# One hybrid encoder layer with 16 experts: bank waits, residual products and x by column halves rearranged, four more expert chunks loaded in the mixing stage

## The chip, the core and the metric

The kernel runs on one core of one Trainium2 chip. The metric is the device time of one execution in microseconds (us); the runs of the kernel before have a median of 499.74 us. TensorE is called PE, VectorE DVE, ScalarE ACT, GpSimd POOL and SyncE SP, as in the profile.

## What is computed

One layer over 256 tokens of width 1024, batch 1, in float32. Three mixers (differential attention, causal pooling, a chunked scan) read one normed projection; their gated sum goes through an output product; then cross attention to 256 memory tokens, and a mixture of 16 experts of which each token takes two.

```python
h = rmsnorm(x, g_mix);  proj = h @ w_in                       # 1024 x 6408
merged = (gates[:, :, 0] * (o_a @ w_branch[0]) + gates[:, :, 1] * (o_b @ w_branch[1])
          + gates[:, :, 2] * (o_c @ w_branch[2]))
x = x + merged @ w_mix_out
x = x + mem_cross_attention(rmsnorm(x, g_xattn), rmsnorm(mem, g_mem), w_xq, w_xkv, w_xo)
x = x + hierarchical_moe(rmsnorm(x, g_moe), ...)              # top-1 group, top-2 expert in it
return rmsnorm(x, g_final)

for e in range(N_EXPERTS):                                    # in hierarchical_moe
    a = jax.nn.silu(hf @ w_gate[e]) * (hf @ w_up[e])
    y = y + comb_dense[:, e:e + 1] * (a @ w_down[e])
```

## The kernel before

Everything is written out by hand: each engine has its own program, and semaphores join them. Nothing is scheduled by a planner.

**Dense stages.** The dense weights come as 80 chunks of up to 512 KB, in the order of the list `BLOCKS`: q, k, v, bcd, xs, pool, z, six gate blocks g0 to g5, the branch products b10 to b21 with the memory keys mka, then m0 and m1 (the output product of the mixers), mkb, xq, mv, xo0, xo1. SP loads chunk n into one of four buffers `raw`. ACT rounds it to fp32r (`wh`, line 622), DVE subtracts that from the raw chunk (`wl`, line 1006), and PE makes three products for each piece (lines 1585 to 1587: high x high, low x high, high x low). `wh` and `wl` have four buffers too. For chunks 0 and 1 the halves are split one by one (`head_hi`, `head_lo`, line 1101), so that the first product can start on half a chunk.

**The start.** x arrives as two DMAs, 128 tokens each with all 1024 columns. PE first multiplies constants (`WARM[0]` = 13 times, line 1596), then transposes the 16 tiles of x (line 1618), where the first tokens' eight come before any of the second tokens'; a transpose of the gains g_mix stands among them (line 1617). Six more warming products follow (line 1592), then chunk 0. ACT and DVE make the high and low parts of the gained columns from the transposes.

**Banks.** Block b of `BLOCKS` sums into the PSUM banks 0 and 1 or 2 and 3 in turn. At a block's first chunk PE waits until both banks of the pair are free (semaphores `free`). In the branch blocks DVE drains a bank by `gates = (gates + 1) * bank` (line 1323) and, outside b10 and b11, adds the result to the sum (line 1326). It waits for its own first instruction, then signals the bank as free with an instruction of its own.

**Experts.** 192 chunks of expert weights (512 KB, two a unit, 96 units) go through 38 buffers (`HOMES`), most of them places that earlier stages no longer need. SP alone issues them, in order. `EARLY` = 9 of them are issued between dense loads, from mka on. The next four go to the part of `gates` that is free once the merged rows are transposed, and are issued after the last dense chunk's load. Later ones wait, each for what frees its place: the products of m1, the last dense chunks, the router's products, and for the places in x the semaphores `x_kept` (PE has copied the residual x into PSUM by products with the identity, `keep_residual`, line 1919) and `moe_rows` (DVE has made the rows for the experts, line 1392). From chunk 38 on each load waits until PE has used up the unit that lay there (lines 1985, 1986 for gate and up, 2003, 2013 and 2039 for down).

**The residual products.** `keep_residual(t, half)` makes a 128x512 product in float32. Two stand after the router's second folded product and before PE waits for the chosen experts, one after the rank products, and one in the first expert's first unit.

**The end.** ACT makes the columns 0 to 511 of the normed output (line 950), DVE the others (line 1578). SP stores tokens 0 to 127 and ACT tokens 128 to 255, 512 KB each.

Of the kernel before, what the change touches and what calls it, by code (L numbers as in the profile page):

```python
# [9 lines left out]
ALU = mybir.AluOpType  # L10
# [3 lines left out]
P = 128  # L14
# [36 lines left out]
EARLY = 9  # L51
RAWG = 16
# [81 lines left out]
WARM = (13, 0, 6, 6, 0, 0, 0, 0)  # L134
# [4 lines left out]
def program(nc, a, out):  # L139
    ctx = ExitStack()  # L140
    with ctx:
# [268 lines left out]
        def _(sp):  # L410
            sp.dma_start(x[:, 0, :], a["x"][0, 0:P, :]).then_inc(s_("x_in0"), 16)
            sp.dma_start(x[:, 1, :], a["x"][0, P:S, :]).then_inc(s_("x_in1"), 16)
# [38 lines left out]
            for n, (name, c, src, kn, cols) in enumerate(CHUNK):  # L451
# [8 lines left out]
                else:  # L460
                    sp.dma_start(dst, src).then_inc(arrived[n % RAW], 16)
                later_parameters(n)
# [23 lines left out]
                if 0 <= n - FIRST["mka"] < EARLY:  # L486
# [3 lines left out]
                    load_chunk(n - FIRST["mka"], n - FIRST["mka"], UNITS)  # L490
            chunks = [2 * u + j for u in ORDER for j in range(2)]
            for at in range(EARLY, len(chunks)):
# [5 lines left out]
                if at < RAWX:  # L498
                    free_by = HOMES[slot][1]
                    if free_by == "mixed":  # L500
                        sp.wait_ge(s_("cols_pe"), COLS["mix"] + 4)
# [32 lines left out]
            sp.wait_ge(s_("final_rows"), 1)  # L534
            sp.wait_ge(s_("final_rows_act"), 1)
            sp.dma_start(out[0, 0:P, :], scaled[:, 0, :]).then_inc(stored, 16)
            sp.wait_ge(stored, 16 * T)
# [64 lines left out]
        def _(act):  # L602
# [87 lines left out]
            act.wait_ge(s_("head_in"), 16)  # L690
            head_hi(0, 0, s_("head_hi"))
# [11 lines left out]
            for t in range(T):  # L703
                square_sum(x[:, t, :], h_ss[:, t:t + 1], hm[:, t, :], s_("sum_squares"))
            for n in range(CHUNKS):
                if n + LEAD < CHUNKS and n != FIRST["mv"]:
                    split(n + LEAD)
                name = BLOCK_AT.get(n)
# [242 lines left out]
            act.wait_ge(s_("final_rows_act"), T)  # L951
            act.wait_ge(s_("final_rows"), T)
            act.dma_start(out[0, P:S, :], scaled[:, 1, :]).then_inc(stored, 16)
# [3 lines left out]
        def _(dve):  # L957
# [138 lines left out]
            def head_lo(n, half):  # L1096
# [3 lines left out]
                dve.wait_ge(hi, n + 1)  # L1100
# [8 lines left out]

            head_lo(0, 0)  # L1110
# [8 lines left out]
            for t in range(T):  # L1119
                mean_square(h_ss[:, t:t + 1], D, h_ss[:, t:t + 1], "h", t)  # L1120
            for n in range(CHUNKS):
                if n == 1:

# [192 lines left out]
                if name and name[0] == "b" and name != "bcd":  # L1316
                    b, half = int(name[1]), int(name[2])
                    dve.wait_ge(s_("gate_tanh"), 12)
                    for t in range(T):
# [3 lines left out]
                        link(dve.scalar_tensor_tensor(out=gt, in0=gt, scalar=1.0, in1=bank[j][:, :], op0=ALU.add, op1=ALU.mult))  # L1323
# [258 lines left out]
        def _(pe):  # L1582
# [29 lines left out]
            for t in range(T):  # L1612
                pe.wait_ge(s_(f"x_in{t}"), 16)
                for kt in range(KD):
# [5 lines left out]
                    if t and kt % 2:  # L1620
                        mm.then_inc(s_("cols_pe"), 1)
# [562 lines left out]
```

## Time and profile before

| | us |
|---|---|
| runs, median (lowest, highest) | 499.74 (499.23, 500.0) |
| the profiled execution | 498.48 |
| its span, from first to last instruction | 496.4 |
| PE busy | 482.4 |
| DVE busy | 256.4 |
| ACT busy | 193.3 |
| moved by DMA | 149.28 MB, 301 GB/s over the span |

The span is the part of the time that the trace shows; 2.1 us of the profiled execution lie outside it. A busy PE in the profile is one whose matmuls follow each other closely; whether it waited is seen from the distance between the starts of two matmuls. In the timeline a product in float32 stands as two instructions.

### The profile page before, as it was taken

How to read it: one execution, taken by the hardware profiler on the slowest of the kernel's cores; microseconds unless marked ns; L12 is line 12 of the kernel's file. 1: busy time of each engine (PE TensorE's matmuls, PEld its weight loads, DVE VectorE, ACT ScalarE, POOL GpSimd, SP SyncE). 2: the span in 40 equal slices, each digit the busy share in tenths (PEclk: the TensorE clock that was granted, in tenths of full speed). 3: DMA queues.
4: the chain of work that ended last, by engine and by line, in shares of the span. 5: the costliest groups of instructions: out<-in, count | busy, mean ns of one | idle time of the engine just before them, and what ended most of it. 6: DMA issues, size and time to landing. Idle time of an engine off the chain costs nothing.

```text
span 496.4 us, 7021 instructions
## 1 busy us (share of the span) xinstructions
PE 482.4 (97%) x2708; PEld 326.0 (66%) x2708; DVE 256.4 (52%) x495; ACT 193.3 (39%) x342; POOL 15.7 (3%) x30
## 2 busy tenths in 40 slices
PE   9999999999999999999999999999999999999983
PEld 9998998888888888788996534433443344333331
DVE  3784799888788689985675531111121111211113
ACT  5645566466626555445675212111111121111113
POOL 1000000000120000000100000000000000000000
PEclk9999999999999999999999999999999999999997
DMA  7897676463346648887799999999999999999992
GB/s 257 271 322 230 193 257 191 127 187 108 105 174 199 169 128 296 296 312 233 265 407 401 332 409 403 400 411 408 409 409 409 408 409 410 409 409 400 398 372 96
DMA packets 63658, 149.28 MB, mean 301 GB/s; under 512 B 8774, under 2 KB 15108, under 8 KB 63620
## 3 DMA queue, kind: packets, MB, share of 16 engines
q1 hardware_dynamic: 63460, 148.24, 82.1%
q8 instruction: 24, 0.39, 0.3%
q10 hardware_dynamic: 160, 0.53, 0.3%
q14 instruction: 14, 0.11, 0.1%
HBM read 147.69 MB, written 1.05 MB: 300 GB/s over the span
## 4 chain that ended last, share of the span: by engine, by line
PE 50%; issue 45%; DVE 3%; ACT 0%; POOL 0%; POOLq 0%; DVEq 0%; ACTq 0%
PE bank L1585 14%; PE bank L1586 13%; PE bank L1587 13%; PE bank L1608 1%; PE bank L1596 1%; DVE wl L1006 1%; PE bank L1706 1%; PE bank L1729 1%; PE bank L1702 1%; DVE gates L1323 1%; PE bank L1896 0%; PE bank L1874 0%; PE bank L1856 0%; PE bank L1618 0%; PE bank L1825 0%
## 5 line engine op out<-in xcount | busy, mean ns | idle before, releaser
L622 ACT ACTIVATE wh<-raw 128x1024 fp32r<-128x1024 f32 (+2 forms) x82 | 82.3, 1021 | 62.9 <-PE bank L1587 47.1
L1006 DVE TENSOR_TENSOR wl<-raw,wh 128x1024 fp32r<-128x1024 f32 (+1 forms) x78 | 91.9, 1195 | 24.9 <-ACT wh L622 23.4
L1585 PE MATMUL bank<-wh,ah 128*128 128x512 f32 (+2 forms) x248 | 95.2, 384 | 0.9 <-issue 0.8
L1586 PE MATMUL bank<-wl,ah 128*128 128x512 f32 (+2 forms) x248 | 93.3, 376 | 0.0
L1587 PE MATMUL bank<-wh,al 128*128 128x512 f32 (+2 forms) x248 | 93.3, 376 | 0.0
L1585 PEld LDWEIGHTS bank<-wh,ah 128*128 128x128 f32 x248 | 46.7, 188 | 10.0 <-issue 1.3
L1587 PEld LDWEIGHTS bank<-wh,al 128*128 128x128 f32 x248 | 46.6, 188 | 8.6
L1586 PEld LDWEIGHTS bank<-wl,ah 128*128 128x128 f32 x248 | 46.7, 188 | 7.8
L1585 PE MATMUL bank<-ah,wh 128*128 128x256 f32 x160 | 45.6, 285 | 0.0
L1586 PE MATMUL bank<-al,wh 128*128 128x256 f32 x160 | 45.3, 283 | 0.0
L1587 PE MATMUL bank<-ah,wl 128*128 128x256 f32 x160 | 45.3, 283 | 0.0
L1500 DVE SCALAR_TENSOR_TENSOR y_lo<-bank,ant,y_hi 128x512 fp32r<-128x512 f32 x15 | 11.3, 750 | 61.1 <-ACT y_hi L885 61.1
L885 ACT ACTIVATE y_hi<-bank,ant 128x512 fp32r<-128x512 f32 x15 | 10.3, 687 | 53.1 <-PE bank L2013 27.0
L1495 DVE TENSOR_TENSOR kT<-bank,kT 64x512 f32<-64x512 f32 x8 | 5.5, 688 | 49.1 <-ACT kT L880 49.1
L1586 PEld LDWEIGHTS bank<-al,wh 128*128 128x128 f32 x160 | 30.7, 192 | 0.1
L1585 PEld LDWEIGHTS bank<-ah,wh 128*128 128x128 f32 x160 | 30.6, 192 | 0.1
L1587 PEld LDWEIGHTS bank<-ah,wl 128*128 128x128 f32 x160 | 30.6, 192 | 0.0
L1495 DVE TENSOR_TENSOR normg<-bank,normg 64x512 f32<-64x512 f32 x8 | 5.5, 689 | 40.8 <-ACT normg L880 40.8
L880 ACT ACTIVATE kT<-bank 64x512 f32<-64x512 f32 x8 | 4.7, 593 | 49.1 <-PE bank L1986 49.1
L880 ACT ACTIVATE normg<-bank 64x512 f32<-64x512 f32 x8 | 4.7, 592 | 47.1 <-PE bank L1986 47.1
L1986 PE MATMUL bank<-wh_raw,expert_cols 128*64 128x512 f32 x48 | 21.9, 593 | 0.0
L1985 PE MATMUL bank<-wl_raw,expert_cols 128*64 128x512 f32 x44 | 20.1, 593 | 0.6 <-DMA raw<-in_w_exp_up 0.6
(402 smaller groups left out, 902.6 us busy)
## 6 DMA issues: line engine op xcount, KB each, us to landing
raw<-in_w_in SPq DMA_DIRECT2D x47, 512.0 KB, 4.9
gates<-in_w_exp_down SPq DMA_DIRECT2D x13, 512.0 KB, 11.4
raw<-in_w_branch SPq DMA_DIRECT2D x12, 512.0 KB, 4.2
wh_raw<-in_w_exp_up SPq DMA_DIRECT2D x12, 512.0 KB, 13.4
raw<-in_w_exp_up SPq DMA_DIRECT2D x11, 512.0 KB, 14.7
wl_raw<-in_w_exp_gate SPq DMA_DIRECT2D x11, 512.0 KB, 12.7
gates<-in_w_exp_gate SPq DMA_DIRECT2D x9, 512.0 KB, 14.5
wl_raw<-in_w_exp_down SPq DMA_DIRECT2D x9, 512.0 KB, 14.1
```

The source lines that it names most:

```text
L622: act.activation(dst, src, ACT.Copy, scale=scale).then_inc(done, 1)
L880: act.activation(act_pair[n // 2 % 2][row_half[n % 2], :], src[r, :], ACT.Silu).then_inc(s_("gate_silu"), 1)
L885: act.activation(yh[:, :], src[:, :], ACT.Copy, scale=combs[:, p % 2:p % 2 + 1]).then_inc(s_("y_hi"), 1)
L1006: dve.tensor_tensor(wl[:, n % RING, 0:sz], raw[:, n % RING, 0:sz], wh[:, n % RING, 0:sz].bitcast(F32), ALU.subtract)\
L1323: link(dve.scalar_tensor_tensor(out=gt, in0=gt, scalar=1.0, in1=bank[j][:, :], op0=ALU.add, op1=ALU.mult))
L1495: dve.tensor_tensor(rows, src[r, :], rows, ALU.mult).then_inc(s_("act_rows"), 1)
L1500: dve.scalar_tensor_tensor(out=dst, in0=src, scalar=combs[:, p % 2:p % 2 + 1], in1=hi.bitcast(F32), op0=ALU.mult, op1=ALU.subtract).then_i ...
L1585: pe.matmul(dst, st[0], mv[0], start=start, stop=False, skip_group_check=True)
L1586: pe.matmul(dst, st[0], mv[1], start=False, stop=False, skip_group_check=True)
L1587: return pe.matmul(dst, st[1], mv[0], start=False, stop=stop, skip_group_check=True)
L1985: pe.matmul(dst[gate, :], st, gw[:, kk, :], start=(kt == 0), stop=(kt == KD - 1), skip_group_check=True)
L1986: mm = pe.matmul(dst[up, :], st, uw[:, kk, :], start=(kt == 0), stop=(kt == KD - 1), skip_group_check=True)
```

## The change

- x comes as two DMAs by column halves, both token tiles each. The first half is the first DMA; the second is issued after chunk 1's load.
- PE transposes the eight tiles of the first half before chunk 0 (the gains first), and the other eight after chunk 0. There are 10 warming products in place of 13, and 5 in place of 6.
- The first half of chunk 0 is rounded by DVE, no longer by ACT.
- ACT's two squares of x for the norm move behind the split of chunk 3, and DVE's two small steps on them to the loop's second turn.
- In blocks whose banks hold the two token tiles (all but q, k, xs, pool, mka, mkb, xq), PE waits for the first bank before the first tile's products and for the second bank before the second tile's.
- DVE's drain of a branch bank signals the bank as free with the drain itself, and waits on that.
- Four expert chunks (`MIXED` = 4) are issued between the dense loads of m1's last chunk, mkb and xq, each in the place after one load.
- The residual products are cut into quarters of 256 columns: one between the two folded products, six before the wait for the chosen experts, one after the rank products, none in the expert loop.
- The output is stored as four DMAs of 256 KB, all by SP, in the order in which the halves are made.

```diff
-WARM = (13, 0, 6, 6, 0, 0, 0, 0)
+WARM = (10, 5)
...
-            sp.dma_start(x[:, 0, :], a["x"][0, 0:P, :]).then_inc(s_("x_in0"), 16)
-            sp.dma_start(x[:, 1, :], a["x"][0, P:S, :]).then_inc(s_("x_in1"), 16)
+            x_rows = a["x"][0].rearrange("(t p) d -> p t d", p=P)
+            sp.dma_start(x[:, :, 0:512], x_rows[:, :, 0:512]).then_inc(s_("x_in0"), 16)
...
+                if EARLY < n - FIRST["mka"] <= EARLY + MIXED:
+                    at = n - FIRST["mka"] - 1
+                    sp.wait_ge(s_("cols_pe"), COLS["mix"] + 4)
+                    load_chunk(at, at, UNITS)
             chunks = [2 * u + j for u in ORDER for j in range(2)]
-            for at in range(EARLY, len(chunks)):
+            for at in range(EARLY + MIXED, len(chunks)):
...
-                        link(dve.scalar_tensor_tensor(out=gt, in0=gt, scalar=1.0, in1=bank[j][:, :], op0=ALU.add, op1=ALU.mult))
-                        dve.sem_inc(free[j], 1)
+                        dve.scalar_tensor_tensor(out=gt, in0=gt, scalar=1.0, in1=bank[j][:, :], op0=ALU.add, op1=ALU.mult).then_inc(free[j], 1)
+                        dve.wait_ge(free[j], NAMES.index(name) // 2 + 1)
...
-                if c == 0 and b >= 2:
+                by_rows = not (name in ("q", "k", "xs", "pool", "mka", "mkb", "xq"))
+                if c == 0 and b >= 2 and not by_rows:
                     for half in range(2):
                         pe.wait_ge(free[2 * (b % 2) + half], b // 2)
...
                     for t in range(T):
+                        if c == 0 and b >= 2:
+                            pe.wait_ge(free[2 * (b % 2) + t], b // 2)
                         mm = rows_out(banks[t][:, 0:cols], t, 0, cols, True)
```

SP at the start, before and then after: `x` is the input, `raw` the dense chunks.

```order
L411 DMA x<-in_x 128x1024
L412 DMA x<-in_x 128x1024
L458 DMA raw<-in_w_in 128x512
L459 DMA raw<-in_w_in 128x512
L461 DMA raw<-in_w_in 128x2x512 x3
```

```order
L413 DMA x<-in_x 128x2x512
L459 DMA raw<-in_w_in 128x512
L460 DMA raw<-in_w_in 128x512
L462 DMA raw<-in_w_in 128x2x512
L464 DMA x<-in_x 128x2x512
L462 DMA raw<-in_w_in 128x2x512 x2
```

The second 512 KB of x moved behind chunk 1.

SP from the load of m1's last chunks on, before and then after: the rows on `gates` are expert chunks, those on `raw` dense ones.

```order
L461 DMA raw<-in_w_mix_out 128x2x512 [waits lo_done] x2
L461 DMA raw<-in_w_xkv 128x8x128 [waits lo_done]
L461 DMA raw<-in_w_xq 128x4x256 [waits lo_done] x2
L461 DMA raw<-in_w_xkv 128x4x256 [waits lo_done] x2
L461 DMA raw<-in_w_xo 128x2x512 [waits lo_done] x2
L449 DMA gates<-in_w_exp_up 128x1024 [waits cols_pe]
L449 DMA gates<-in_w_exp_gate 128x1024 [waits cols_pe]
L449 DMA gates<-in_w_exp_up 128x1024 [waits cols_pe]
L449 DMA gates<-in_w_exp_gate 128x1024 [waits cols_pe]
L449 DMA ah_raw<-in_w_exp_up 128x1024 [waits chunk_used]
```

```order
L462 DMA raw<-in_w_mix_out 128x2x512 [waits lo_done] x2
L450 DMA gates<-in_w_exp_up 128x1024 [waits cols_pe]
L462 DMA raw<-in_w_xkv 128x8x128 [waits lo_done]
L450 DMA gates<-in_w_exp_gate 128x1024 [waits cols_pe]
L462 DMA raw<-in_w_xq 128x4x256 [waits lo_done]
L450 DMA gates<-in_w_exp_up 128x1024 [waits cols_pe]
L462 DMA raw<-in_w_xq 128x4x256 [waits lo_done]
L450 DMA gates<-in_w_exp_gate 128x1024 [waits cols_pe]
L462 DMA raw<-in_w_xkv 128x4x256 [waits lo_done] x2
L462 DMA raw<-in_w_xo 128x2x512 [waits lo_done] x2
L450 DMA ah_raw<-in_w_exp_up 128x1024 [waits chunk_used]
```

Four expert loads moved ahead of four dense ones; those behind keep their order and their waits.

PE from the router's folded products (`pr`) to the first expert's second unit, before and then after: `x,ident` are the residual products, `ant,consts` the rank products, `sel` the gathers.

```order
L1915 MATMUL bank<-pr 128x20 x2
L1919 MATMUL bank<-x,ident 128x512 x2
L1949 MATMUL bank<-ant,consts 128x32
...
L1953 MATMUL bank<-ant,consts 128x16
L1919 MATMUL bank<-x,ident 128x512
L2066 MATMUL bank<-sel,rows_hi 128x256 x4
...
L1986 MATMUL bank<-o_rows,expert_cols 64x512
L1919 MATMUL bank<-x,ident 128x512
L1963 MATMUL bank<-sel,rows_hi 128x256 x2
```

```order
L1929 MATMUL bank<-pr 128x20
L1935 MATMUL bank<-x,ident 128x256
L1929 MATMUL bank<-pr 128x20
L1935 MATMUL bank<-x,ident 128x256 x6
L1964 MATMUL bank<-ant,consts 128x32
...
L1968 MATMUL bank<-ant,consts 128x16
L1935 MATMUL bank<-x,ident 128x256
L2081 MATMUL bank<-sel,rows_hi 128x256 x4
...
L2001 MATMUL bank<-o_rows,expert_cols 64x512
L1978 MATMUL bank<-sel,rows_hi 128x256 x2
```

A whole product left the expert loop, half of one left the place behind the ranks, and both stand ahead of the ranks now.

## Rows read from the trace of the kernel before

**Rows 1.** The page: busy us of each engine, and GB/s in 40 slices.
```profile
PE 482.4 (97%) x2708; PEld 326.0 (66%) x2708; DVE 256.4 (52%) x495; ACT 193.3 (39%) x342; POOL 15.7 (3%) x30
...
GB/s 257 271 322 230 193 257 191 127 187 108 105 174 199 169 128 296 296 312 233 265 407 401 332 409 403 400 411 408 409 409 409 408 409 410 409 409 400 398 372 96
```

**Rows 2.** Windows: us, PE, PEld, DVE, ACT, POOL busy (x), PEclk, DMA share, GB/s.
```profile
220.00:230.00 10.00, 10.00 (x46) 8.27 (x45) 7.72 (x12) 5.48 (x9) 0.00 (x0) 1.00 0.73 231
...
280.00:285.00 5.00, 5.00 (x30) 2.83 (x30) 0.46 (x2) 2.52 (x6) 0.00 (x0) 1.00 0.72 234
```

**Rows 3.** Timeline of the start: start us, us, engine, instruction, [idle before <-releaser].
```profile
1.05 5.51 PE L1596 MATMUL bank<-consts 128*128 128x128 f32 x26 [1.05 <-POOL consts L551]
...
7.12 0.63 ACT L622 ACTIVATE wh<-raw 128x512 fp32r<-128x512 f32 x1 [4.20 <-DMA raw<-in_w_in]
...
8.15 0.68 DVE L1101 TENSOR_TENSOR wl<-raw,wh 128x512 fp32r<-128x512 f32 x1
...
8.45 1.50 PE L1592 MATMUL bank<-ident 128*128 128x128 f32 x12
...
9.13 0.87 DVE L992 SCALAR_TENSOR_TENSOR al<-bank,consts,ah 128x256 fp32r<-128x256 f32 x2 [0.31 <-ACT ah L622]
...
9.51 0.84 ACT L622 ACTIVATE ah<-bank,consts 128x256 fp32r<-128x256 f32 x2
...
9.76 0.35 PE L1585 MATMUL bank<-ah,wh 128*128 128x256 f32 x1
```

**Rows 4.** Timeline of DVE around the low part of chunk 4.
```profile
17.98 2.27 DVE L1126 COPY pr<-pr 4x165 f32<-4x165 f32 x31
20.18 2.46 DVE L1006 TENSOR_TENSOR wl<-raw,wh 128x1024 fp32r<-128x1024 f32 x2
```

**Rows 5.** Timelines of PE and DVE in the branch blocks.
```profile
193.17 1.09 PE L1608 MATMUL bank<-ident,hm 128*128 128x128 f32 x8 [0.16 <-DVE al L999]
...
207.33 0.68 DVE L1323 SCALAR_TENSOR_TENSOR gates<-gates,bank 128x512 f32<-128x512 f32 x1
...
208.64 0.28 PE L1587 MATMUL bank<-ah,wl 128*128 128x256 f32 x1
209.72 0.47 PE L1585 MATMUL bank<-wh,ah 128*128 128x512 f32 x1 [0.81 <-issue]
```

**Rows 6.** Timeline of PE around the rank products and in the first expert.
```profile
270.92 1.96 PE L1919 MATMUL bank<-x,ident 128*128 128x512 f32 x4
...
273.55 0.41 PE L1949 MATMUL bank<-ant,consts 128*128 128x32 f32 x2 [0.67 <-DVE ant L1428]
...
279.40 1.12 PE L1919 MATMUL bank<-x,ident 128*128 128x512 f32 x2
```

**Rows 7.** SP's waits from 270 to 290, and the landing of x's two chunks.
```profile
SPq L449 <- PE bank L1919: 3.3, 1, 3.3
...
SPq L520 <- DVE rows_lo L1392: 2.2, 1, 2.2
...
DMA to landing us min/median/max: 4.2/4.7/5.2
```

**Rows 8.** Timeline of PE in the last experts, at each unit's first product.
```profile
465.20 0.61 PE L1985 MATMUL bank<-wl_raw,expert_cols 128*64 128x512 f32 x1
...
467.76 0.61 PE L1985 MATMUL bank<-wl_raw,expert_cols 128*64 128x512 f32 x1 [0.62 <-DMA raw<-in_w_exp_up]
...
473.09 0.64 PE L2003 MATMUL bank<-wl_raw,pr 128*64 128x512 f32 x1 [0.17 <-DMA wh_raw<-in_w_exp_down]
```

**Rows 9.** Timeline of ACT where the four loads are put.
```profile
228.19 1.06 ACT L622 ACTIVATE wh<-raw 128x1024 fp32r<-128x1024 f32 x1 [1.66 <-PE bank L1587]
```

**Rows 10.** The stores: both issues, and from issue to landing.
```profile
491.30 0.36 SPq L536 DMA_DIRECT2D out<-scaled  x1
491.85 0.38 ACTq L953 DMA_DIRECT2D out<-scaled  x1
...
DMA to landing us min/median/max: 3.5/3.8/4.1
```

More of the change, by code:

```diff
@@ L51 @@
 EARLY = 9
+MIXED = 4
 RAWG = 16
@@ L533, in _ @@
                         load_chunk(c % RAWG, c, SPILL_UNITS)
[L534 to L537, printed above, removed]
+            for t in range(T):
+                for half, ready in ((1, s_("final_rows")), (0, s_("final_rows_act"))):
+                    c = slice(512 * half, 512 * half + 512)
+                    sp.wait_ge(ready, t + 1)
+                    sp.dma_start(out[0, P * t:P * t + P, c], scaled[:, t, c]).then_inc(stored, 16)
+            sp.wait_ge(stored, 16 * 2 * T)
         @block.gpsimd
@@ L707, in _ @@
                     split(n + LEAD)
+                if n == 0:
+                    for t in range(T):
+                        square_sum(x[:, t, :], h_ss[:, t:t + 1], hm[:, t, :], s_("sum_squares"))
                 name = BLOCK_AT.get(n)
@@ L1610, in to_cols, with x_cols @@
                     mm.then_inc(s_("cols_pe"), 1)
-            for t in range(T):
-                pe.wait_ge(s_(f"x_in{t}"), 16)
-                for kt in range(KD):
-                    if t and kt == KD // 2:
-                        pe.wait_ge(s_("gains_in"), 16)
-                        pe.transpose(bank[0][:, 0:KD], g_rows[:, :], ident[0:KD, 0:KD]).then_inc(s_("early_T"), 1)
-                    mm = pe.transpose(rest[kt // 2][:, 256 * (kt % 2) + P * t:256 * (kt % 2) + P * t + P],
-                                      x[:, t, P * kt:P * kt + P], ident[:, :])
-                    if t and kt % 2:
+            def x_cols(part):
+                pe.wait_ge(s_(f"x_in{part}"), 16)
+                for kt in range(4 * part, 4 * part + 4):
+                    for t in range(T):
+                        mm = pe.transpose(rest[kt // 2][:, 256 * (kt % 2) + P * t:256 * (kt % 2) + P * t + P],
+                                          x[:, t, P * kt:P * kt + P], ident[:, :])
+                    if kt % 2:
                         mm.then_inc(s_("cols_pe"), 1)
+            pe.wait_ge(s_("gains_in"), 16)
+            pe.transpose(bank[0][:, 0:KD], g_rows[:, :], ident[0:KD, 0:KD]).then_inc(s_("early_T"), 1)
+            x_cols(0)
             def chunk(n):
@@ L1915, in folded, with keep_residual @@
                 return pe.matmul(bank[2][:, 20 * t:20 * t + 20], parts[:, t, :], fold[:, 0:20], start=True, stop=True, skip_group_check=True)
-            def keep_residual(t, half):
-                mm = pe.matmul(rest[2 * t + half][:, :], ident[:, :], x[:, t, 512 * half:512 * half + 512], start=True, stop=False,
-                               skip_group_check=True)
-                if t and half:
+            def keep_residual(t, *quarters):
+                for q in quarters:
+                    c = slice(256 * (q % 2), 256 * (q % 2) + 256)
+                    mm = pe.matmul(rest[2 * t + q // 2][:, c], ident[:, :], x[:, t, 256 * q:256 * q + 256], start=(q % 2 == 0), stop=False,
+                                   skip_group_check=True)
+                if t and 3 in quarters:
                     mm.then_inc(s_("x_kept"), 1)
```

37 lines of the change are left out of this document (16 added, 21 removed).

## The prediction, as it was written before the changed kernel ran

> **What bounds the kernel now.** I read the page first [rows 1]: PE is busy 97% of the span, and the DMA rate lies between 105 and 320 GB/s in the first half and at 400 to 410 from slice 21 on. So there are two candidates, PE and, from 260 us on, the expert weights. Neither share says which one binds, since a busy PE may still wait for short. I therefore went through the starts of the dense products. They follow each other at 0.12 us (256 columns) or 0.23 us (512 columns) nearly everywhere up to 268 us; the places where they don't are few, and the largest is at 209.72 [rows 5]. The dense stages are PE's, and what comes earlier on PE there stays earlier. In the experts a unit of 1 MB takes PE four pairs of products, 0.43 us apart, 1.72 us in all, and takes the DMA 2 x 512 KB / 409 GB/s = 2.56 us; but gathers, scatters, transposes and the second halves of the row-wise down products, which need no new weights, lie between the units. PE starts far behind the stream and eats its lead up. It is stopped by a landing only at the very end, at 467.76 and 473.09 [rows 8]. So both bind together at the end: PE up to there, the stream of chunks after that. A gain on one alone is worth no more than what is left on the other.
>
> **The start.** The 26 instructions of the 13 warming products take 5.51 us, 0.21 each, and hold x's transposes back to 6.4 us; ten products end near 1.05 + 20 x 0.21 = 5.3. The gains' transpose and eight transposes of x are done near 6.6, five warming products (rate of the row at 8.45: 0.125 an instruction) end near 7.8. On the other side stands the first half of chunk 0: it landed at 7.1, behind 1 MB of x. Now it is behind 0.5 MB, which at 409 GB/s is 1.3 us less, 5.8. DVE's new rounding has no row in the trace; the nearest are ACT's of the same form, 0.63, and DVE's own subtraction of that size, 0.68; I take 0.6, and both ends change nothing, since 5.8 + 0.6 + 0.68 for the low part + 0.43 for one low column part make 7.5 us, so PE is ready at 7.8 and not at 9.76 [rows 3]. But the second eight transposes (0.9 us) now follow chunk 0 (2.9 us), and behind them ACT needs, in order, two column parts 0.84, chunk 2 1.08, two more 0.84, chunk 3 1.08, two squares of the size of a rounding 2.1, chunk 4 1.1 [rows 3, 9]; DVE follows with its 2.27 us of table copies after the second square, then the low part of chunk 4, 1.2 [rows 3, 4]. From the transposes' pair at 11.2 that gives 17.3 for the squares, 17.6 to 19.9 for the copies, 21.1 for chunk 4's low part, where the kernel before has 21.4. PE, ready at 20.5, waits for it. **Gain 0.6**, not 2; from 1.1, if DVE gets there sooner, to a loss of 1.0, if x's second half lands after 10.7.
>
> **The branch blocks.** At 209.72 PE stood 0.96 us: its last product began at 208.64 and one takes 0.12. It waited for both banks. DVE's drain of the first ended at 207.33 + 0.68 = 208.01; the second's is two DVE instructions later, and PE started at 209.72 with its end [rows 5]. Now the first tile's six products (6 x 0.23 = 1.39 us) need only the first bank, start at 208.76 and end at 210.15, after the second is free. **Gain 0.96**, all of it, for the transposes of the merged rows stand behind a whole chunk and DVE has their sums done by then. If DVE came later, part of it would turn up as a wait there: 0.6 to 0.96. The other blocks show no such gap; there a satisfied wait moves from a chunk's start to its middle, at no cost, as the chunk starts with their waits show no longer distance. The drain loses one semaphore instruction, some 0.06 us, ten times in a stretch in which DVE has no idle time; PE waits for that chain once, at 193.17 (0.55 after a product that takes 0.23) [rows 5]. **Gain 0.2**, between 0 and 0.3.
>
> **The residual products.** A full product is 0.86 us (four instructions in 1.96 with overlap), a quarter 0.21. The one between the folded products holds up the second by about 0.2: loss 0.2, on the chain to the chosen experts. The six behind it, 2.6 us, end near 273.7, where the ranks now begin (273.55 + 0.2). Behind the ranks PE waits for DVE's selection anyway. In the expert the product at 279.40 goes: 0.9 [rows 6]. **Gain 0.7** (0.5 to 0.9) for PE from there on.
>
> **The four chunks.** They take 4 x 1.28 = 5.1 us of the stream. They go where the DMA has room: share 0.73, 231 GB/s [rows 2]; four more chunks in 20 us make that some 335. The dense loads behind each land 1.3 us later, and ACT, when it takes one up, has been waiting 1.66 us for PE and not for the load [rows 9]. Cost 0; if a load were so late that nothing covered it, 1.3 once, which the low parts' lead over PE would still have to let through. What does the stream gain? Not 5.1: most chunks wait for their places. SP, which wanted to load into x, stood 2.2 us for DVE's rows and then 3.3 more for the residual product at 279.40; the DMA share fell to 0.72, and x's first chunk landed 4.2 us after its issue at 280.5 [rows 2, 7]. With that product gone only the other condition is left, met at 280.5 - 3.3 = 277.2, so the issue comes 3.3 us earlier; and because four chunks are already in, nothing is queued ahead of it that would hold it up. From there on each load follows used units, which PE frees faster than 2.56 us. The stream gains 3.3 of its own, plus 0.6 + 0.96 + 0.2 - 0.2 that come to it from PE: 4.9. PE gains 0.6 + 0.96 + 0.2 + 0.7 = 2.5. So the stream outruns PE by 2.4, and PE's stops at the end go: from 465.20 to the next unit's 467.76 pass 2.56 us for 1.72 of products, 0.84, and the unit before and the one at 473.09 were held by some 0.1 and 0.35 [rows 8]. **Gain 1.3.** That needs the two edits together: PE 2.5 + 1.3 = 3.8 is still under the stream's 4.9.
>
> **The stores.** Before, SP issues at 491.30, ACT at 491.85, and the second 512 KB land 4.1 us later, at 496.0 [rows 10]. SP waited for ACT's half, DVE's comes first; an issue takes SP 0.36. So four issues 0.4 to 0.45 apart run from 491.05 to 492.4; the last is 256 KB and lands, by the 3.5 of the first store less the 0.6 of the halved size, near 495.2. **Gain 0.8**, between 0 and 1.2.
>
> The Trainium skill, DMA: Bandwidth & Descriptors, Anatomy of one DMA, gives a fixed 2.0 us plus bytes at 436 GB/s, and by an estimate from that page the last quarter would land at 495.0, close to mine. Its section Bandwidth asks for 1 MiB or more in one DMA, which speaks against quarters; the trace has 512 KB chunks at 409 GB/s when many are in flight, which does not agree for transfers that overlap.
>
> **Sum.** 0.6 + 0.96 + 0.2 + 0.7 + 1.3 + 0.8 = 4.6. The span goes from 496.4 to 491.8, the profiled execution from 498.48 to 493.9. It lay 1.26 under the median of the runs, so the forecast for the median is 499.74 - 4.6 = **495.1**.
>
> **The rivals.**
> The start gives nothing: the second half of x or DVE's longer list holds chunk 4 back. For it: the chain of ACT and DVE has no slack, and each 0.1 us of it counts. Against: less is ahead of chunk 0. Then 495.7, down to a loss of 1.0, 496.7.
> The stream stays late: the gap at 280 us only moves, because x's places need DVE's rows or used units. Then the stops at the end stay, and the end comes by the stream's own gain, 1.6, plus 0.8 for the stores: 497.3. Against it: the wait for PE's line 1919 is the longest there, and it ends with that line.
> The stores don't gain: four small transfers each pay their latency. 495.9. The rule on transfers of 1 MiB is this rival, and it could cost more if they didn't overlap.
> Slower: the clock. The warming instructions start at 0.21 us and the same form takes 0.125 at 8.45 [rows 3]; PE goes from the lower level (1.2 GHz) to the higher (2.4 GHz) within the warm-up. If PE now stands idle between its shorter warm-up and x's first half, the rise comes later and dense products take twice their 0.12. Each us at the lower level costs 0.5; slower than before by the 1.0 us that count needs 5.6 us lost, so 11 us at the lower level. Then above 500.7. Against: x landed before the warm-up ended.
> The Trainium skill, TensorE: Matmul & The Clock Gate, What's actually happening, says that the low clock is the default and sustained activity lifts it; the two rates agree.
>
> **Chances.** Forecast, all six terms within their bounds, 0.62 (494.0 to 496.1); the start gives nothing 0.13; the stream stays late 0.10; the stores 0.05; two of these together, within a microsecond of before, 0.05; slower 0.05. The range from 493.4 to 497.5 takes in the first four and their bounds. About 0.2%, 1.0 us, is what a measurement of this kernel can tell from no change: faster 0.90, same 0.05, slower 0.05.
>
> **What the profile after would show.** First dense product near 7.8 us and chunk 4's first product near 21.1; no gap over 0.3 us at the second branch block of b2; ranks about 1.6 us earlier and not 1.8; no residual product in the expert loop; x's chunk issued near 275.5; DMA share near 0.9 at 220 to 240 and idle time somewhere in 245 to 275; no idle before a unit's first product after 440 that a DMA ended; four stores some 0.4 apart. The forecast is wrong if chunk 4 starts no earlier, or if a landing still stops PE after 440.

## The result, and the profile after

The changed kernel takes 495.56 us (median of six runs, 495.09 to 496.75) beside 499.59 for the kernel before: 4.0 us less, ratio 0.9921, 95% interval 0.9902 to 0.9940. Run again with the experiments it gave 495.87, ratio 0.9922 (0.9908 to 0.9936). The forecast was 495.1, 493.4 to 497.5. The profiled execution took 495.11 us with a span of 493.4.

That span is 3.0 us shorter than the one shown of before, although the times differ by 4.0. The execution of before whose profile is shown was a quick one: its span is 496.4, and the median span of 21 later executions was 497.8. One pair of traces is therefore not enough here to say where 4 us went. With the experiments there are 14 traces, and the parts are compared over all of them below.

The page of the changed kernel, rows as in [rows 1]:

```profile
PE 481.5 (98%) x2708; PEld 326.8 (66%) x2708; DVE 257.0 (52%) x496; ACT 192.7 (39%) x341; POOL 15.7 (3%) x30
...
GB/s 259 276 301 247 194 263 192 129 183 97 114 184 187 183 129 259 332 319 343 244 342 394 399 401 406 401 410 408 410 410 407 410 410 408 411 408 399 397 350 91
```

PE is busy for 0.9 us less in 3.0 us less span: mainly idle time went. The dip to 332 GB/s in slice 23 has gone, and slices 17 to 19 carry more (332, 319, 343 for 296, 312, 233).

The start, timeline of PE and DVE, to be held against [rows 3]:

```profile
1.05 4.64 PE L1602 MATMUL bank<-consts 128*128 128x128 f32 x20 [1.05 <-POOL consts L558]
...
5.82 1.57 PE L1623 MATMUL bank<-ident,x 128*128 128x128 f32 x8
...
6.06 0.43 DVE L1115 CAST wh<-raw 128x512 fp32r<-128x512 f32 x1
...
8.54 0.36 PE L1591 MATMUL bank<-ah,wh 128*128 128x256 f32 x1
...
11.48 1.04 PE L1623 MATMUL bank<-ident,x 128*128 128x128 f32 x8
...
21.14 0.60 PE L1771 MATMUL bank<-ident,small 128*128 128x128 f32 x4
21.50 0.36 PE L1591 MATMUL bank<-ah,wh 128*128 128x256 f32 x1
```

The first dense product begins 1.22 us earlier (9.76 before), chunk 4 only 0.21 (21.71 before). The first eight transposes take 1.57 us, 0.2 each: TensorE's granted clock rises from 1.2 to 2.4 GHz only at 6.84 us in this trace (5.98 in the trace of before). The second eight, now behind chunk 0, take 1.0 us of PE that they did not take at that place before.

The second branch block and the expert stage, timelines of PE (compare [rows 5, 6, 8]):

```profile
208.05 0.28 PE L1593 MATMUL bank<-ah,wl 128*128 128x256 f32 x1
208.17 0.40 PE L1591 MATMUL bank<-wh,ah 128*128 128x512 f32 x1
...
272.19 0.37 PE L1964 MATMUL bank<-ant,consts 128*128 128x32 f32 x2
...
470.01 0.64 PE L2018 MATMUL bank<-wl_raw,pr 128*64 128x512 f32 x1 [0.16 <-DMA wh_raw<-in_w_exp_down]
```

The gap of 0.96 is gone: 208.17 follows 208.05 by one product's 0.12. The ranks start 1.36 us earlier. One landing still stops PE near the end, for 0.16 us (0.17 at the same place before); the stop of 0.62 at the unit of 467.76 is gone.

Windows, as in [rows 2]:

```profile
220.00:230.00 10.00, 10.00 (x46) 8.29 (x45) 6.65 (x10) 5.12 (x8) 0.00 (x0) 1.00 0.92 309
...
240.00:250.00 10.00, 10.00 (x85) 9.40 (x84) 5.96 (x10) 6.79 (x13) 1.66 (x1) 1.00 0.71 244
...
280.00:285.00 5.00, 5.00 (x28) 2.24 (x26) 2.47 (x13) 1.77 (x5) 0.00 (x0) 1.00 1.03 402
```

SP's waits from 270 to 290, to be held against [rows 7]:

```profile
SPq L450 <- PE bank L2001: 8.4, 6, 2.2
SPq L450 <- PE bank L1968: 3.7, 1, 3.7
SPq L525 <- DVE rows_lo L1398: 2.2, 1, 2.2
```

The residual product no longer holds SP. x's first chunk is issued at 275.86 (280.55 before) and lands at 281.31 (284.77): 4.7 us earlier to issue, 3.5 to land. The last expert chunk lands at 480.79 (483.83).

The stores, SP's row for the four issues, and the DMA rate in 40 slices from 487 to 494 us:

```profile
487.72 2.75 SPq L543 DMA_DIRECT2D out<-scaled  x4
...
GB/s 0 0 0 0 0 0 0 94 0 316 339 386 386 363 363 363 293 35 23 59 363 351 410 386 375 386 386 304 35 35 23 12 0 0 0 0 0 0 0 0
```

The issues are at 487.72, 488.13, 488.60 and 490.04. The first three have drained by about 490, and for half a microsecond almost nothing moves before the fourth's data does.

### The profile page after: what moved, and what is told of

It is laid out like the page before. It is cut to its first block, busy times and chain, and to the rows that moved or that the text cites. A ratio compares the mean times of both kernels' runs of the same rounds, so it can differ in the third digit from the quotient of the medians.

```text
span 493.4 us, 7009 instructions
## 1 busy us (share of the span) xinstructions
PE 481.5 (98%) x2708; PEld 326.8 (66%) x2708; DVE 257.0 (52%) x496; ACT 192.7 (39%) x341; POOL 15.7 (3%) x30
## 3 DMA queue, kind: packets, MB, share of 16 engines
HBM read 147.69 MB, written 1.05 MB: 301 GB/s over the span
## 4 chain that ended last, share of the span: by engine, by line
PE 54%; issue 44%; DVE 0%; ACT 0%; POOL 0%; POOLq 0%; ACTq 0%
PE bank L1591 15%; PE bank L1593 15%; PE bank L1592 15%; PE bank L1614 1%; PE bank L1602 1%; PE bank L1718 1%; PE bank L1741 1%; PE bank L1714 1%; PE bank L1623 0%; PE bank L1910 0%; PE bank L1870 0%; PE bank L1839 0%; PE bank L1879 0%; PE bank L1846 0%; PE bank L1838 0%
## 5 line engine op out<-in xcount | busy, mean ns | idle before, releaser
L2001 PE MATMUL bank<-raw,expert_cols 128*64 128x512 f32 x44 | 20.3, 594 | 0.0
```

The costliest lines, as they stand in the source:

```text
L2001: mm = pe.matmul(dst[up, :], st, uw[:, kk, :], start=(kt == 0), stop=(kt == KD - 1), skip_group_check=True)
```

## The experiments

Twelve more traces were taken, one of them of the changed kernel again. Since the time of one kernel spreads by 1 to 2 us over its executions, and the medians of 5 runs by several tenths, each is judged by its trace at the place that its edit touches, and by its time only where the difference is large. The table has, from each trace in us: the time at which the granted clock rises to 2.4 GHz; the start of the first dense product and of chunk 4; from mka's product to m0's (the second branch block lies between); from the first product of chunk xo1, the last dense one, to the landing of the 151st expert chunk issued, to the last landing, and to the start of PE's last product; from there to the end of the span; and the median time with its ratio to before.

```
kernel                  rise first chunk4 mka-m0  151st   last PE end  tail   time  ratio
before                  5.98  9.76  21.71  10.27 165.47 219.66 223.70  8.53 499.88 1
e6_before_chunks        6.31  9.92  21.86  10.31 165.49 219.81 223.87  9.88 499.22 0.9991
e12_before_bank_waits   6.98 10.24  22.19   9.23 165.58 219.81 223.85  9.65 499.02 0.9988
e7_before_residual      7.05 10.27  22.22  10.30 163.64 218.77 222.87  9.87 498.33 0.9969
e9_old_start_and_drain  6.79 10.15  22.09   9.23 163.16 218.20 222.22  9.35 497.40 0.9955
e2_residual_in_expert   4.58  7.63  20.60   9.23 165.48 219.89 223.61  9.57 496.98 0.9958
e1_no_chunks            5.81  8.08  21.04   9.24 163.74 218.94 222.84  9.26 495.74 0.9922
changed (first trace)   6.84  8.54  21.50   9.24 163.23 218.22 221.94  8.87 495.56 0.9921
a0_after (second)       5.96  8.12  21.08   9.23 163.11 218.20 221.93  9.88 495.87 0.9922
e4_banks_at_start       6.91  8.54  21.49   9.61 163.42 218.11 221.81  9.42 495.78 0.9919
e8_quarters_two_queues  4.68  7.69  20.65   9.23 163.17 218.86 222.70  9.63 495.67 0.9913
e3_two_stores           4.17  7.67  20.63   9.23 163.19 218.66 222.49  9.44 494.97 0.9905
e10_copies_later        6.29  8.29  21.26   9.24 163.11 217.93 221.62  9.38 494.94 0.9911
e11_all_three           4.56  7.71  20.66   9.23 163.24 217.93 221.71  9.25 494.73 0.9913
```

### The expert stream: which edit closed the gap?

e1_no_chunks:

```
-MIXED = 4
+MIXED = 0
...
+                    if free_by == "mixed":
+                        sp.wait_ge(s_("cols_pe"), COLS["mix"] + 4)
```

> The changed kernel with its four extra chunks back behind the dense loads, all else as changed. Theory 1, as the prediction has it (the gap of the stream at 280 us closes only because four chunks are already in): without them the stream keeps only PE's 1.6 us, the last landing moves from 480.8 to about 482.2 and the span from 493.4 to about 494.8. Theory 2 (the residual product alone held the stream up, and the four chunks only move idle DMA time from 278-283 to 245-257): the last landing stays within 0.4 us of 480.8 and the span within 0.4 us of 493.4.

e2_residual_in_expert:

```
             folded(0)
-            keep_residual(0, 0)
             folded(1).then_inc(s_("logits_pe"), 1)
-            keep_residual(0, 1, 2, 3)
-            keep_residual(1, 0, 1, 2)
+            keep_residual(0, 0, 1, 2, 3)
...
-            keep_residual(1, 3)
+            keep_residual(1, 0, 1)
...
                 if n == 0:
+                    keep_residual(1, 2, 3)
```

> The changed kernel with the residual products where they were (one quarter pair of them behind the first expert unit). Theory 1 (the product at 279 us keeps x's places, and with them the stream, back): x's first chunk is issued at 279.0 instead of 275.9 and lands at 283.1 or later instead of 281.3, the last landing comes 1.8 us later, near 482.6, and the span is near 495.2. Rival (with four chunks ahead the stream no longer needs x's places in time): the landings stay, PE alone loses 0.65, the span is near 494.05 or, where the end still waits for landings, 493.4.

e7_before_residual is the kernel before with keep_residual and its calls as changed, and nothing else:

> The kernel before with the residual products alone rearranged. Theory 1 (the gap of the stream closes only with the four chunks): x's chunk is issued earlier, but the last landing stays near 483.8 and the time within 0.5 us of before. Theory 2 (the product at 279 us alone kept the stream back): the last landing comes 2.0 to 2.6 us earlier, near 481.5, PE's waits for landings at the end go, and the time is 1.5 to 2.0 us under before (ratio 0.996 to 0.997).

e6_before_chunks is the kernel before with the MIXED loads and nothing else:

> The kernel before with the four chunks alone put between the dense loads. Both theories: the residual product at 279.4 us still keeps x's chunk to 280.5, the stream only idles longer ahead of it, the last landing stays within 0.4 us of 483.8 and the time within 0.5 us of before (ratio 0.999 to 1.001). Rival (the lead that four early chunks give lasts): the last landing comes 1 us or more earlier and the time is 1 us lower.

The four kernels make a square. With neither edit, or with the chunks alone, the 151st chunk lands 165.5 us after xo1 (four traces, 165.47 to 165.58). With the residual products alone it is 163.7 (two traces), with both 163.2 (eight traces, 163.11 to 163.42). So the residual products are worth 1.8 us to the stream by themselves, the chunks nothing by themselves and 0.5 on top of the residual products. For PE's last product it is 223.76, 222.86 and 222.05 in the mean: 0.9 for the residual products alone, 0.8 more with the chunks. The times agree on the residual products: e7 is 1.5 us under before, e2 1.1 over a0_after (its eight executions spread from 496.06 to 499.41), and e6 within 0.7 of before, with an interval (0.9979 to 1.0002) that takes in no change. The chunks' 0.8 at PE's end is not shown: it is two traces against eight, two of the eight (222.49, 222.70) lie within 0.4 of the two (222.84, 222.87), and the time of e1, 495.74, is no longer than the changed kernel's.

In e2 SP waits for the residual product again, as in [rows 7]; x's first chunk is issued at 278.04 and lands at 282.47 (in a trace that starts its first dense product 0.9 earlier than the changed kernel's, so 3.1 and 2.1 later at the same start), and the DMA idles:

```profile
SPq L450 <- PE bank L1935: 3.3, 1, 3.3
...
280.00:285.00 5.00, 5.00 (x28) 2.11 (x26) 2.69 (x15) 1.53 (x3) 0.00 (x0) 1.00 0.99 340
```

In the kernel before with the residual products alone the idle time is nearly gone without any early chunk (392 GB/s, 234 in [rows 2]), but PE still meets the landing near the end:

```profile
PE bank L1988 <- DMA raw<-in_w_exp_up: 0.6, 1, 0.6
...
280.00:285.00 5.00, 5.00 (x30) 2.89 (x30) 0.58 (x2) 2.52 (x6) 0.00 (x0) 1.00 1.05 392
```

The same wait of 0.6 stands in e1 and in e2. With both edits it stands in two of eight traces (e3 and e8, which have the latest last landings of the eight) and is gone in six; six of eight against none of two is too few to show that the chunks remove it. So e2's theory 1 stands: 1.8 later forecast, 1.6 measured at the last landing. For e1 and e7 neither theory came out whole. The residual products make most of the stream's gain without the chunks (theory 2), but PE's stop near the end was gone only with both (theory 1), and then not in every execution; in e7 the last landing came 1.0 earlier against xo1, where theory 2 had 2.0 to 2.6.

### The bank waits and the drain

e12_before_bank_waits, the kernel before with:

```
-                if c == 0 and b >= 2:
+                if c == 0 and b >= 2 and not by_rows:
...
                     for t in range(T):
+                        if c == 0 and b >= 2:
+                            pe.wait_ge(free[2 * (b % 2) + t], b // 2)
```

> The kernel before with the bank waits alone by rows, the drain of DVE as it was. As the prediction has it, the waits alone take away the gap of 0.96 at the second branch block: from mka.0 to m0.0 pass 9.3 us instead of 10.27. Rival (the changed kernel with its waits back at the chunk's start took 9.61 there, so most of the gap belonged to the drain's semaphore instruction): 9.9. Time 0.4 to 0.9 us under before.

e4_banks_at_start, the same edit taken back in the changed kernel:

> The changed kernel with both bank waits at a chunk's start again. Theory 1 (the gap at the second branch block is on the path of both PE and the stream): the gap of 0.96 us is back near 208.2, every dense start behind it and the last landing come 0.9 to 1.0 us later, span 494.3. Rival (the saturated stream sets the end and takes it up): m0 starts 0.96 later, but the last landing stays at 480.8 and the span within 0.3 of 493.4.

Alone on the kernel before, the waits by rows take the block from 10.27 to 9.23: 1.04, as the prediction has it, and e12's rival falls. Taken back in the changed kernel they cost only 0.37:

```profile
208.03 0.28 PE L1593 MATMUL bank<-ah,wl 128*128 128x256 f32 x1
208.44 0.47 PE L1591 MATMUL bank<-wh,ah 128*128 128x512 f32 x1
```

PE waits there 0.29, not 0.96, since the shorter drain frees both banks earlier. The two edits cover the same gap: either alone is worth 0.7 to 1.0 there, both 1.03. My expectation for e4 had overlooked that; its time, 0.1 under a0_after, cannot tell 0.4 from nothing.

### The start, and the drain by itself

e9_old_start_and_drain:

```
-WARM = (10, 5)
+WARM = (13, 6)
...
+            act.wait_ge(s_("head_in"), 16)
+            head_hi(0, 0, s_("head_hi"))
...
-            dve.wait_ge(s_("head_in"), 16)
-            link(dve.tensor_copy(wh[:, 0, 0:512], raw[:, 0, 0:512]))
...
-                        dve.scalar_tensor_tensor(out=gt, in0=gt, scalar=1.0, in1=bank[j][:, :], op0=ALU.add, op1=ALU.mult).then_inc(free[j], 1)
-                        dve.wait_ge(free[j], NAMES.index(name) // 2 + 1)
+                        link(dve.scalar_tensor_tensor(out=gt, in0=gt, scalar=1.0, in1=bank[j][:, :], op0=ALU.add, op1=ALU.mult))
+                        dve.sem_inc(free[j], 1)
```

and x's two loads by token tiles with all 16 transposes ahead of chunk 0, the squares ahead of chunk 3's high part, as before.

> The changed kernel with two parts undone that lie 180 us apart, so that one trace shows both by place: x again by token tiles with the 13 warming products and the old order of ACT and DVE at the start, and DVE's drain of a bank again with a semaphore instruction of its own. Start: over three traces of the old start chunk 4 begins at 21.7 to 22.2, over seven of the new one at 20.6 to 21.5. Theory 1 (the new start is worth 0.9 on average, and the 0.3 us that the time keeps outside the span belong to it): chunk 4 at 21.7 to 22.2 here, and time less span back from 1.77 to 2.1. Rival (the start is worth the 0.2 of the first pair of traces): chunk 4 within 0.3 of 21.5. Drain: from chunk b00.1 to b01.0 pass 4.39 us in the changed kernel and 4.76 before; here 4.76 again, and, since the by-row waits cover it, from mka.0 to b21.0 no more than 2.9 to 3.1. Time: 1.3 to 1.6 us over the changed kernel, 497.0 to 497.4.

Chunk 4 starts at 22.09 and the time outside the span is 2.08 us again. Over five traces of the old start chunk 4 begins at 22.01 in the mean, over nine of the new one at 20.99: 1.0 us, and 0.3 more outside the span (1.73 to 1.82 with the new start, 2.08 to 2.09 with the old). But the two sets did not have the same clock: it rose at 5.98 to 7.05 in the five, 6.6 in the mean, and at 4.17 to 6.91 in the nine, 5.5 in the mean. In four of the nine it rose before 4.7 us, when PE had done nothing yet but warming products that the kernel before makes too, so PE's changed work is unlikely to have brought that on. Traces with the same rise give the size of the edit:

| clock rises at | chunk 4, old start | chunk 4, new start |
|---|---|---|
| 5.96 to 6.31 | 21.71, 21.86 | 21.08, 21.26 |
| 6.79 to 7.05 | 22.09, 22.19, 22.22 | 21.50, 21.49 |

That is 0.6 to 0.7; the other 0.3 to 0.4 of the 1.0 go with earlier rises in the traces taken. So of theory 1 the 0.3 outside the span stand and its 0.9 do not, and the rival's 0.2 was low because the first trace of before had an early rise for its kind, that of after a late one.

From b00.1 to b01.0 pass 4.77 us: the drain's semaphore instruction costs 0.38 there, and between mka and m0, behind the waits by rows, nothing. One such instruction takes 0.11 us of DVE: from a drain's start to the addition behind it pass 0.82 to 0.84 us, eight times in each of the five traces that have it, and 0.71 to 0.72 in the nine that don't. Before and after:

```profile
208.15 0.69 DVE L1326 TENSOR_TENSOR gates<-gates 128x512 f32<-128x512 f32 x1
```

```profile
206.22 0.68 DVE L1330 SCALAR_TENSOR_TENSOR gates<-gates,bank 128x512 f32<-128x512 f32 x1
206.94 0.69 DVE L1333 TENSOR_TENSOR gates<-gates 128x512 f32<-128x512 f32 x1
```

The drain ahead of the addition at 208.15 began at 207.33 [rows 5]. The time of e9 is 1.5 over a0_after; 0.6, 0.3 and 0.38 make 1.3.

e10_copies_later:

```
                 if n == 1:
...
+                if n == 2:
                     dve.wait_ge(s_("table_in"), 16)
                     for lo, hi, b in bucket_runs():
```

> The changed kernel with DVE's 31 table copies (2.27 us) one chunk later, behind the low part of chunk 4 instead of ahead of it. Theory (this list on DVE, and not x's transposes or the rounding, sets chunk 4 in the changed kernel): from chunk 3 to chunk 4 pass 2.9 us instead of 3.24, and everything behind is 0.35 earlier against the first dense product; time 0.3 to 0.4 under the changed kernel. Rival (ACT's squares set it, or DVE is late by as much one chunk later): 3.24 stay, or turn up from chunk 4 to 5.

The rival, and more: from chunk 3 to chunk 4 pass 3.24 us in every trace, old or new, with the copies ahead or behind. Neither DVE nor ACT sets this. Between the two chunks PE has four transposes of its own:

```profile
21.02 0.28 PE L1593 MATMUL bank<-ah,wl 128*128 128x256 f32 x1
21.14 0.60 PE L1771 MATMUL bank<-ident,small 128*128 128x128 f32 x4
```

I had taken chunk 4's start as set by DVE's low part, which ends shortly before it [rows 4]; the 0.36 us ahead of the chunk are PE's own work. From the first dense product to chunk 4 PE never waits for long: 11.94 or 11.95 us in each trace of the old start, 12.95 to 12.97 in each of the new, the difference being the eight transposes that moved in between. Chunk 4 gains what the first product gains, less 1.0. Its time, 494.94 beside 495.87 of a0_after, has nothing in the trace to stand on, and shows how far medians of five wander.

e11_all_three takes the copies later, 8 warming products and two stores:

```
-WARM = (10, 5)
+WARM = (8, 5)
```

> As the one with the copies later, and the warm-up of 8 products instead of 10, and the output in two stores of 512 KB from SP and ACT. Theory on the warm-up (with ten it ends at 5.6 us where the clock has not risen by then, though x's half landed at 5.2): x's transposes start at 5.3, and in executions with a late rise of the clock chunk 0 comes up to 0.4 earlier. Rival (less activity ahead lets the clock rise later, after 7.1 us, and each us at the lower level costs 0.5): chunk 0 no earlier than 8.1. Stores: as in the kernel with two stores, 0 to 0.9 under the quarters. Time: 494.3 to 495.3.

Its first product comes at 7.71, in a trace with an early rise of the clock, where kernels with ten warming products have 7.63 to 7.69. What it does in an execution with a late rise was not seen, so the question of the shorter warm-up stays open.

### The stores

e3_two_stores:

```
-            for t in range(T):
-                for half, ready in ((1, s_("final_rows")), (0, s_("final_rows_act"))):
...
+            sp.dma_start(out[0, 0:P, :], scaled[:, 0, :]).then_inc(stored, 16)
...
+            act.dma_start(out[0, P:S, :], scaled[:, 1, :]).then_inc(stored, 16)
```

> The changed kernel with the output in two stores of 512 KB, one from SP and one from ACT, as before. As forecast, four quarters gain 0.8: then the span here is 494.2 and the time 0.8 us over the changed kernel's. Rival (in the changed kernel's trace the fourth store was issued 1.4 us after the third, at 490.04, and the gain over before behind PE's last product was nil): span 493.4, no difference.

> The changed kernel again, for a second trace of it and for the comparison with its relatives. It should lie at 0.991 to 0.992 of the time before (495.2 to 495.8), with a last landing of 480.4 to 481.0. Forecast for the stores (four quarters are worth 0.8): it is 0.8 us faster than the one with two stores of 512 KB. Rival (the quarters are worth nothing, or cost the latency of the last one): it is no faster than that one, or up to 0.6 us slower.

e8_quarters_two_queues gives SP only the two quarters that DVE scales, and lets ACT issue its own two:

> The changed kernel with the four stores shared out: SP stores DVE's two quarters, ACT its own two. Theory (in three of four traces the fourth store on SP's queue was issued 1.4 to 2.1 us after the third, and that eats the gain of the quarters): all four issues lie within 1.3 us of the first, the last landing comes 5.2 us or less after ACT's first scaling instead of 5.8 to 6.5, and the time is 0.7 us under the changed kernel's. Rival (1 MB at some 409 GB/s plus the latency sets the end, whatever the queue): no difference within 0.3 us.

From PE's last product to the end pass 9.44 us in the mean with two stores (six traces, 8.53 to 9.88), 9.39 with four from SP (seven, 8.86 to 9.88), 9.63 with four from two queues. The quarters gain nothing that the traces show. In e8 all four issues lie within 0.8 us of the first, and still the last landing comes 6.6 us after ACT's first scaling, where its theory had 5.2 or less: its rival stands. By the times two stores are 0.9 faster than four, but the intervals (0.9892 to 0.9918, 0.9908 to 0.9936) overlap; that the quarters cost something is not shown. The rates of the DMA from 487 to 494 us, first of a0_after, then of e3_two_stores, with the code load that falls into both:

```profile
GB/s 0 0 0 0 0 0 117 351 339 374 351 351 503 363 363 316 386 374 363 363 374 374 117 23 23 35 23 23 23 23 35 23 23 23 23 0 0 0 0 0
...
q8 instruction: 1, 0.02, 1.0%
```

```profile
GB/s 0 0 0 0 0 0 0 94 281 374 374 351 351 398 468 351 398 374 421 374 374 374 398 94 47 23 23 23 23 23 23 23 23 0 0 0 0 0 0 0
...
q8 instruction: 1, 0.02, 1.3%
```

The bulk of the 1 MB has gone about 3.6 us after the first issue, at some 370 GB/s. Then 23 GB/s are left, a sixteenth of that, for 2.1 and 1.6 us, so one DMA engine is behind the other fifteen. A block of 16 KB of code went over one engine ahead of that, beside the stores, and took it 1.1 and 1.5 us. That this block is what put the engine behind, and that no cut of the output would alter it, fits and was not tested. The Trainium skill, DMA: Bandwidth & Descriptors, section on why a DMA increments its semaphore by 16, says that the engines of one DMA finish independently and that only all sixteen together mean landed; the trace agrees: the rate of a0_after fell at 491.0, and its last store landed at 493.55, when the last engine was done. Four issues on one queue have a price of their own: in five of seven traces SP issued the fourth 1.4 to 2.1 us after the third, and in those the code load began 0.7 to 0.95 us after the first issue; in the two where it began 1.2 and 1.8 us after it, the fourth followed in 0.5. That the load held SP up is the likeliest reading, and was not tested.

## Why the prediction was right, point by point

**The total** fell 4.0 where 4.6 was forecast. With the start at equal clock the parts make 0.6 + 0.3 (start, and outside the span) + 1.03 (bank waits) + 0.38 (drain) + 1.7 (residual products, chunks and the stops at the end) + 0.05 (stores) = 4.1. The timed runs give 3.2 to 4.6 by the second interval. For the profiled pair the same parts within the span are 0.21 + 1.03 + 0.38 + 1.76 - 0.34 = 3.04, the 3.0 of the spans. Part of the closeness is luck: the stores' 0.8 did not come, and 0.3 outside the span and 0.2 more from the drain, neither of them forecast, made up for 0.5 of it. One of the two signs by which the forecast called itself wrong did show: a landing still stops PE after 440, for 0.16 us.

**The start, 0.6.** Measured 0.2 in the first pair, 1.0 in the mean, 0.6 to 0.7 at an equal rise of the clock, and 0.3 outside the span. The size was right by a wrong way: no chain of ACT and DVE holds chunk 4 (e10), PE does. The first product was forecast for 7.8 and comes at 7.6 to 8.5, 1.6 to 1.7 ahead of the old start at an equal rise; 1.0 of that goes to the transposes behind it.

**The bank waits, 0.96.** Measured 1.04 alone (e12): the step was right. What it had not seen is that the drain's edit would have taken away 0.66 of the same gap by itself (10.27 to 9.61).

**The drain, 0.2.** Measured 0.38: all of it ahead of b01, where PE waits for DVE. The term was set too low, and its bound of 0.3 too: it priced the instruction at 0.06 us, and one takes 0.11.

**The residual products, 0.7.** From 1.60 us ahead of before at xo1 PE was 2.25 ahead at the second expert unit: 0.65. The first unit is 1.41 ahead, so the 0.2 lost on the second folded product is there too.

**The stream, 4.9.** At the 43rd chunk it was 3.55 ahead, at the 151st 3.85, at the last 3.04. The step that failed is that nothing would be queued ahead of x's chunk: at 275.86 the three chunks ahead were still on their way, the last of them until 280.40, so an issue 4.7 us earlier became a landing 3.5 earlier. And the idle time did not vanish, it went forward: 244 GB/s from 240 to 250, 342 before, where the chunks wait for places that PE frees. The stream on its own gained 2.3 (165.5 to 163.2), not 3.3.

**The stops at the end, 1.3.** From 2.25 ahead to 3.36 at PE's last product: 1.1 in the first pair. The mean over the traces with both edits is 1.7 for this and the residual products together, where 2.0 was forecast. A stop by a landing remains, of 0.16 in the changed kernel's traces and of 0.65 and 0.78 in all in two of its relatives. The rest was lost in the last landing: a landing is that of the slowest DMA engine, and at the end of the longer unbroken stream the engines lie further apart. Rates of the last 4 us up to the last landing, of the kernel before and of a0_after:

```profile
GB/s 420 340 340 400 440 340 380 360 440 340 400 440 440 340 420 380 420 460 280 440 440 300 460 380 380 400 360 300 320 200 360 180 260 240 320 160 240 320 160 240
```

```profile
GB/s 389 369 369 389 389 430 451 348 410 348 430 410 369 410 348 492 410 266 348 225 369 246 205 266 246 266 307 184 246 225 164 307 123 123 82 82 82 82 82 41
```

A sixteenth is some 25 GB/s: before, about nine engines are at work in the last 0.5 us; after, about three. All 14 traces divide this way: 221 to 246 GB/s in the last 0.5 us in the four in which x's chunk waits for the residual product, 25 to 188 in the ten others, while the rate of the stream is the same (405 or 406 GB/s from 20 to 100 us after xo1). The last landing gained 1.5 after xo1, the 151st chunk 2.3. What pulls the engines apart (code loads of 16 KB on one of them every 21 us or so are in both traces) was not isolated.

**The stores, 0.8.** Measured 0.05 in endings that spread by 1.35: the term failed. It took 3.5 us from issue to landing of a 512 KB store, and shortened it with the size to 2.9 for the last quarter. The last quarter lands 2.9 us after its issue only where that issue comes 1.4 to 2.1 late (five traces); where it comes in time it takes 4.3, 4.9 and 5.2 us (e1, a0_after, e8). [rows 10] was also the quickest ending of all fourteen traces (8.53 us, mean 9.4), a poor row to build on.

## What to carry to other kernels

Where several engines and a stream bind in turn, cut the trace at fixed places and compare the same stretch over many traces of related kernels; two single executions differed here by more at the start and in the tail than most edits were worth. A mean over traces is not enough where the two sets differ in something that no edit set: here the rise of the clock, which made 0.6 look like 1.0 until traces with the same rise were compared. Ahead of a step "A waits for B", look for A's own small instructions in the gap: 0.36 us of transposes were taken for slack behind another engine, and a term rested on that. An earlier issue is an earlier landing only as far as the queue ahead of it is empty.

## What the runs showed of the hardware

**The clock rises at a time of its own.** PE does the same warming products from 1.05 us in each trace, and its 128-column instructions stand 0.21 us apart (1.2 GHz) until the pitch falls to 0.11 (2.4 GHz). The granted clock rose at 4.17 us in one trace and at 7.05 in another, and between in the rest. e3_two_stores, early, and the kernel before with the residual products alone, late:

```profile
1.05 3.97 PE L1603 MATMUL bank<-consts 128*128 128x128 f32 x20 [1.05 <-POOL consts L556]
...
5.34 1.09 PE L1624 MATMUL bank<-ident,x 128*128 128x128 f32 x8 [0.16 <-DMA x<-in_x]
...
7.67 0.36 PE L1592 MATMUL bank<-ah,wh 128*128 128x256 f32 x1
```

```profile
1.05 5.92 PE L1596 MATMUL bank<-consts 128*128 128x128 f32 x26 [1.05 <-POOL consts L551]
6.76 1.62 PE L1618 MATMUL bank<-ident,x 128*128 128x128 f32 x12
...
10.27 0.35 PE L1585 MATMUL bank<-ah,wh 128*128 128x256 f32 x1
```

The first dense product moves with it: 7.63 to 8.54 with the new start, 9.76 to 10.27 with the old, and the products up to 190 us keep that shift, within 0.2. Beside the tail, which spreads by 1.35, it is the largest part of the spread between executions that the traces show. The rival of a later rise did not come up: in nine traces of the new start the rise lies at 4.17 to 6.91, in five of the old at 5.98 to 7.05. The Trainium skill, TensorE: Matmul & The Clock Gate, Part 1, describes the monitor's window as free-running, not started by the kernel; a rise at changing times in unchanged instruction streams agrees with that.

**One late DMA engine shows where nothing else moves.** In seven of the fourteen traces (a0_after, e3, e6, e7, e8, e11, e12) the stores end in 1.4 to 2.1 us at 23 to 47 GB/s, the rate of one or two engines. In the five where the fourth issue came late that stretch is 0.7 us. Each trace has one 16 KB block of code on one DMA engine 0.4 to 1.9 us after the first store's issue, which takes it 1.0 to 1.8 us.
